# Causal attentions of the first layer: the diagonal tile's mask and maximum on VectorE in place of mask products on TensorE

## The reference

```python
def query_block(i):
    start = i * Q_BLOCK
    ...
    s = jnp.einsum('bhqd,bhkd->bhqk', q_b, k).astype(F32) * scale
    s = s + c_b[..., :, None] - cum[..., None, :]
    q_pos = start + jnp.arange(Q_BLOCK)
    s = jnp.where(k_pos[None, :] <= q_pos[:, None], s, NEG_INF)
    p = jax.nn.softmax(s, axis=-1)
    return jnp.einsum('bhqk,bhkd->bhqd', p.astype(v.dtype), v)
```

## Time and profile before

| | us |
|---|---|
| median of 3 runs (3127.31 to 3138.06) | 3137.6 |
| the profiled execution: its own time | 3136.82 |
| the profiled execution: span of its trace | 3135.0 |
| start of the first scores and of the last L851, `fa0` | 149.45 and 208.23 |
| the same, `fa1` | 356.90 and 410.39 |
| TensorE busy / VectorE busy / ScalarE busy, whole span | 2808.2 / 855.1 / 652.7 |

### The profile page before, as it was taken

One profiled execution on the slowest core, in us unless ns is written; L12 is line 12 of the kernel. 1 busy time (PEld: TensorE's weight loads), 2 busy tenths in 40 slices (PEclk: granted clock), 3 DMA queues, 4 the chain that ended last, 5 costly groups with the idle time before them and its releaser, 6 DMA issues.

```text
span 3135.0 us, 30943 instructions
## 1 busy us (share of the span) xinstructions
PE 2808.2 (90%) x12510; PEld 1439.4 (46%) x12510; DVE 855.1 (27%) x2227; ACT 652.7 (21%) x1371; POOL 200.6 (6%) x159
## 2 busy tenths in 40 slices
PE   7999977999999599999968989887699998999998
PEld 3454543444444244444443434443455555445454
DVE  2041342112122312203141111110454435145156
ACT  2130331113222100000020011000242334144043
POOL 1000000000000100000010000000201011101101
PEclk9999998999999799999989999999899999999999
DMA  4803238999998521132278999998310211320310
GB/s 171 335 21 135 108 142 334 422 416 424 412 405 352 204 80 54 62 126 81 93 285 351 424 420 424 420 420 338 136 36 14 64 49 55 91 66 23 107 24 34
DMA packets 128344, 639.23 MB, mean 204 GB/s; under 512 B 10448, under 2 KB 26896, under 8 KB 102976
## 3 DMA queue, kind: packets, MB, share of 16 engines
q1 hardware_dynamic: 92928, 541.93, 43.3%
q10 hardware_dynamic: 23536, 51.54, 4.9%
q0 software_dynamic: 11728, 43.66, 3.6%
HBM read 588.80 MB, written 48.23 MB: 203 GB/s over the span
## 4 chain that ended last, share of the span: by engine, by line
PE 70%; DMA 15%; DVE 5%; issue 3%; ACT 2%; PEld 2%; ACTq 1%; PEldq 1%; POOL 1%; SPq 0%; DVEq 0%; POOLq 0%
PE psum L552 15%; PE psum L542 14%; PE psum L1855 9%; DMA ring<-in_expert_w_gu 9%; PE psum L637 7%; PE psum L1867 5%; PE psum L763 5%; DMA arena<-in_expert_w_gu 4%; PE psum L792 3%; PE psum L781 3%; PE psum L992 1%; PE psum L1848 1%; PE psum L2464 1%; PEld psum L2464 1%; PEldq L2931 1%
## 5 line engine op out<-in xcount | busy, mean ns | idle before, releaser
L552 PE MATMUL psum<-ring,XT 128*128 128x512 f32 (+3 forms) x1024 | 410.3, 561 | 4.6 <-DVEq L2931 2.6
L542 PE MATMUL psum<-XT,ring 128*128 128x512 f32 x896 | 387.4, 593 | 3.8 <-DVEq L2931 3.8
L552 PEld LDWEIGHTS psum<-ring,XT 128*128 128x128 f32 x1024 | 193.5, 190 | 216.1 <-issue 197.3
L1855 PE MATMUL psum<-ring,XT 128*64 128x512 f32 x1024 | 244.5, 616 | 27.4 <-DMA ring<-in_expert_w_gu 24.5
L542 PEld LDWEIGHTS psum<-XT,ring 128*128 128x128 f32 x896 | 169.4, 190 | 216.4 <-issue 212.7
L1855 PE MATMUL psum<-arena,XT 128*64 128x512 f32 x1024 | 238.4, 605 | 29.6 <-DMA arena<-in_expert_w_gu 29.6
L637 PE MATMUL psum<-ring,arena 128*128 128x512 f32 x512 | 224.4, 597 | 7.4 <-DVEq L2931 5.0
L763 PE MATMUL psum<-arena 64*128 64x384 f32 (+8 forms) x640 | 198.5, 506 | 27.1 <-ACT arena L817 21.7
L1927 DVE TENSOR_TENSOR XT<-XT,psum 64x512 f32<-64x512 f32 x64 | 44.1, 690 | 538.7 <-ACT XT L1930 538.7
L637 PEld LDWEIGHTS psum<-ring,arena 128*128 128x128 f32 x512 | 96.7, 191 | 127.9 <-issue 116.9
L1855 PEld LDWEIGHTS psum<-ring,XT 128*64 128x64 f32 x1024 | 73.8, 141 | 175.4 <-issue 128.8
(11 more groups left out here) (336 smaller groups left out, 2802.5 us busy)
## 6 DMA issues: line engine op xcount, KB each, us to landing
ring<-in_expert_w_gu SPq DMA_DIRECT2D x64, 2048.0 KB, 17.7
arena<-in_expert_w_gu SPq DMA_DIRECT2D x64, 2048.0 KB, 21.7
arena<-in_expert_w_down SPq DMA_DIRECT2D x32, 2048.0 KB, 14.4
ring<-in_expert_w_down SPq DMA_DIRECT2D x32, 2048.0 KB, 14.3
ring<-in_ada_w SPq DMA_DIRECT2D x12, 2048.0 KB, 9.2
ring<-in_fox_w_in SPq DMA_DIRECT2D x8, 2048.0 KB, 12.6
XT<-xg_dram ACTq DMA_DIRECT2D x32, 512.0 KB, 10.6
y_dram<-XT ACTq DMA_DIRECT2D x128, 128.0 KB, 10.0
```

The lines of the kernel that those rows point to most:

```text
L542: i = pe.matmul(ps[0][0:cols_[1] - cols_[0], 0:ntok], w[:, c, cols_[0]:cols_[1]], x[:, c, tok:tok + ntok], start=(c == 0), stop=(c == k - 1))
L552: i = pe.matmul(ps[0][:, 0:width], x[:, c, t * P:(t + 1) * P], w[:, c, c0:c0 + width], start=(c == 0), stop=(c == k - 1))
L1855: i = pe.matmul(psum[side * BR:(side + 1) * BR, 0:FF], x[:, 4 * part + c, :], w[:, c, side * FF:(side + 1) * FF], start=(part == 0 and c = ...
```

## The change

Both stages use a subclass `Causal`, and `masks_on_pe` is off, so TensorE makes no mask product. VectorE adds the mask to the diagonal tile and takes that tile's maximum in one `tensor_tensor_reduce`, which writes the masked tile back to PSUM. For block 0 the maximum is then only negated; for the others a second reduction takes the negated maximum of the columns ahead of the diagonal, and a `scalar_tensor_tensor` on one column joins the two.

```diff
+        class Causal(Attend):
+
+
+            def maximum(self, dve, n):
+                k, h, i = self.unit[n]
+                neg, top, x = sm[:, 0, n:n + 1], sm[:, 3, n:n + 1], self.s_at(n, i * P, (i + 1) * P)
+                dve_step.then(dve, dve.tensor_tensor_reduce(x, x, self.add(i), 1.0, NEG, ALU.add, ALU.max, top))
+                if i == 0:
+                    return dve.tensor_scalar(neg, top, -1.0, None, ALU.mult)
+                dve_step.then(dve, dve.tensor_reduce(neg, self.s_at(n, 0, i * P), AXX, ALU.max, negate=True))
+                return dve.scalar_tensor_tensor(neg, top, -1.0, neg, ALU.mult, ALU.min)
...
-                Attend(f"fa{g}", 8, NT, lambda i: (0, (i + 1) * P),
+                Causal(f"fa{g}", 8, NT, lambda i: (0, (i + 1) * P),
...
-                       add=lambda i: [(i * P, (i + 1) * P, causal)], masks_on_pe=True)
+                       add=lambda i: causal)
```

## The result

The change makes the kernel slower: 3169.03 us (median of 8 runs, 3150.93 to 3172.53) against 3136.05 us (8 runs, 3127.31 to 3140.36), a ratio of 1.010 with a 95% interval of 1.0089 to 1.0112. The profiled execution took 3169.47 us, its span is 3167.6 us, 32.6 more than before. The mean granted clock over the whole span goes with the time: after the change it is 0.957 in the execution of 3150.93 us and 0.947 in that of 3172.53; in the 85 executions of the kernel before that stand beside the experiments it is 0.960 to 0.966.

What follows compares the result with a forecast made beforehand. TensorE held a 12.71 us pair; afterwards a loop through maximum, exponential, copy and transposes would make VectorE wait. Whole pairs 2.2, drains 1.2, first pairs 1.4 and -2.1 gave +2.7 us: 3140 us, range 3129 to 3151.

Steps and rivals of the forecast that it cites:

- granted clock 1.0 in the pairs: Sign expected in the profile: TensorE at full clock in the pairs of heads of both stages.
- slower by the clock: Rival: TensorE's idling drops its clock to 0.50, +5.2 us a pair, 3166 us with five pairs; chance 0.06.
- The queue: VectorE's instruction queue in both stages: the added mask and maximum work takes 3.7 us more a pair.
- the two waits: VectorE waits at the first maximum of block 1 and of block 2, 0.8 to 1.0 us each.
- the walk: One pair followed from its last unit to the next pair's: 13.26 us against 12.71, 0.55 more a pair.
- the first pair: Start of `fa1`, where only VectorE's queue counts and no loop yet: 1.4 us longer.
- the drain: End of each stage, behind the last pair's first two legs: 0.6 us more per stage, +1.2 together.
- The first pair of `fa0`: Start of the first stage at half clock, where TensorE holds it and about five mask products go: -2.1 us.
- The dear instruction: Rival: the combined instruction takes 0.5 to 0.76 us at 128 columns; 3146 to 3158 us, chance 0.15.
- VectorE never waits: Rival: TensorE without masks runs far enough ahead; a pair takes 11.4 us, the kernel 3132; chance 0.15.
- The whole gain: Rival: VectorE's additions hide and TensorE stays the bound; -14 us, 3124 us, chance 0.04.
- The weighed rule: Waits of VectorE for itself, 14 a pair, would be free, giving 3134 us; rejected, 0.12 us each kept.

Runs made afterwards that it cites:

- e7: e4 with the transposes of even and odd units in two PSUM banks; 3135.34 us, ratio 0.9999.
- e4: Changed kernel with ten extra products to an unread bank behind the fourth unit's scores of each stage; 3145.59 us, ratio 1.0043.
- e6: Kernel before the change with ten extra products to an unread bank at each stage's start; 3136.69 us, ratio 1.0004.
- e2: Kernel before the change without its 64 mask products, so attention is not causal; 3136.19 us, ratio 1.0015.
- e5: Kernel before, mask moved to VectorE as a plain addition then one reduction, plus ten extra products at each stage's start; 3135.56 us, ratio 1.000.
- e13: Changed kernel with the transposes of even and odd units in two PSUM banks and no extra product; 3141.42 us, ratio 1.0024.
- e8: Changed kernel with ten extra products at each stage's start and one per unit, to unread banks; 3143.25 us, ratio 1.0025.

## Why the prediction was wrong

**The step that failed** is the one that left the clock as it was: "granted clock 1.0 in the pairs", and with it the chance of 0.06 for *slower by the clock*. That rival named the place, the price and the time: half clock, five pairs, 3166 us. Measured were 3169, with 40 and 57 us at half clock, which is 4.9 pairs of 19.8 us. Its price per pair was a little low: 18.5 us forecast, 19.8 in the trace. Two things were missed. First, the full clock of `fa1` "behind the same idle time" was taken to speak against it. The idle time was not the same: the prediction looked at VectorE's wait in `fa1`, but TensorE's own was 1.44 us in `fa0` and 1.09 in `fa1`, and the change, which takes four mask products out of it, makes it 2.40 and 2.06. (The row of `fa1` is cut 4 to 8 us behind its first scores, not ten; the clock is 1.00 for the whole stage, so that reading holds.) Second, nothing asked whether the stage gets out of a low clock once it is in it. Before the change TensorE did within about 11 us, with its queue full of mask products; in the two traces after it, 40 to 80 us passed. What holds the clock down for so long stays open.

**The queue** was right in its mechanism. VectorE's additions, the two waits (0.8 to 1.0 forecast, 0.95 and 0.92 found) and their place stand; their cause, the copy, accounts for about half of them (e7). A pair at full clock is 13.03 us (e4), forecast 13.26; the new instruction, 0.30 us in place of 0.36, on the four units of the walk whose maximum lies on the path (4 x 0.06) is enough to account for that. Its price for a stage at full clock is 1.8 us, forecast 3.1 for `fa1`: the first pair 0.7 (1.4 forecast), the two pairs behind it 0.3 each (0.55), the drain 0.5 (0.6), by the first stages of e4 and e6. One sign of the prediction was off without harm: VectorE's busy time in such a pair is 10.39 us, not over 11.5, since its waits for itself do not count as busy.

**The first pair of `fa0`**, -2.1 forecast: from the first scores to the first gating it took 27.1 us, 23.8 before, so +3.3. The half clock did not end in it.

**The dear instruction** is out: 0.30 us. **VectorE never waits** is out: it waits by 1.9 us a pair. **The whole gain** is out, and e2 shows its size: even with no mask anywhere a pair gains 1.27 us, not 1.8, and the clock takes it back.

**The weighed rule**: The Trainium skill, VectorE: DVE Perf Modes, section "The DRAIN you can't avoid", would make the waits for VectorE itself free. In the trace after, the instruction behind a waited-for readout of 0.14 us starts 0.18 after its start (201.00 to 201.18), and behind the unwaited negation of 0.15 it starts after 0.07 (201.18 to 201.25). The difference of 0.11 us a wait stands against the rule here. e5, with 8 such waits in a pair in place of 14, has the shorter pair, but it has fewer instructions too and does not test the waits alone.

**The range** of 3129 to 3151 left out a rival whose top I had worked out myself. With a price of 5 us a pair and eight pairs in the two stages, the clock deserved far more than 0.06.

## What to carry to other kernels

Taking work from TensorE can slow a kernel down when a stage starts after idle time: look at the granted clock by windows of a few us before the change, ask whether the work taken away lay in TensorE's idle time or beside it, and ask of each low stretch what got the engine out of it, not only what put it there. Products to an unread bank tell within one run whether a loss is the clock's. Where one PSUM bank takes every unit's transposes, a second free bank gave more (7 us, no arithmetic changed) than moving the mask in either form did with one bank.

## What the runs showed of the hardware

The granted clock stayed at 0.50 for 40 to 80 us in the changed kernel, while TensorE waited 0.30 us once in a whole pair of 19.8, and for 34 us in e13, where it was busy for 32.00 us of 32.00. The Trainium skill, TensorE: Matmul & The Clock Gate, section "Part 1: The HAM clock gate", says that an engine that is kept busy gets its full clock; these stretches do not agree with it, if busy is what the profile's rows call so.

Gains in clock were not kept one for one. From the second stage's end on, the seven traces with ten products at each stage's start took 2727.2 to 2732.7 us and the ten without 2720.1 to 2727.6. Why the rest of the kernel is longer behind them by some 5 us, though its instructions are the same, stays open; so does part of what e4 and e8 are over before.

`tensor_tensor_reduce` over 128 columns of PSUM takes 0.30 us plus a readout of 0.14 us, no more than the plain `tensor_tensor`; at 512 columns it was 0.07 us more than the plain one.
